# Cached pages on 16 neighbouring partitions with eight rows each, in place of 32 partitions four apart with four rows

## The reference, cut to what matters

```
def diff_core(q1, q2, k1, k2, v, lam, q_pos, k_pos):
    s1 = einsum('bqhd,bkhd->bhqk', q1, k1) * scale      # masked where k_pos > q_pos
    s2 = einsum('bqhd,bkhd->bhqk', q2, k2) * scale
    p1 = softmax(s1); p2 = softmax(s2)
    return einsum('bhqk,bkhd->bqhd', p1 - lam * p2, v)

cache_k_diff  (1, N_PHYS, 128, 4 heads, 128)   paged rotated [k1|k2]
cache_v_diff  (1, N_PHYS, 128, 4 heads, 128)   paged values
page_table    (8 sequences, 16 pages)
```

## Time and profile before

| | us |
|---|---|
| median of 3 runs | 1942.77 (1932.91 to 1943.87) |
| the profiled execution | 1937.89 |
| its span in the profile | 1935.9 |

### The profile page before, as it was taken

How to read it: one execution, slowest core, us unless ns; L and a number is a source line. 1 busy time by engine, 2 the same in 40 slices (tenths; PEclk the granted TensorE clock), 3 DMA queues, 4 the chain that set the end, 5 groups by cost and what they waited for, 6 DMA issues and landing times.

```text
span 1935.9 us, 32623 instructions
## 1 busy us (share of the span) xinstructions
PE 1621.9 (84%) x12772; PEld 770.8 (40%) x12772; DVE 695.8 (36%) x1351; ACT 331.3 (17%) x769; POOL 214.0 (11%) x356
## 2 busy tenths in 40 slices
PE   7999888888897978877787879998978888877784
PEld 3444455555444323222232357764532222223231
DVE  4446578867515200000000169973250000000005
ACT  3100344444302000000000020013110000000001
POOL 1000223322201110110100040000021101011000
PEclk9999999988898998999999989999979999999998
DMA  9995699989754999999999999922279999999995
GB/s 336 358 361 191 230 335 355 364 319 354 298 212 166 368 428 428 412 428 428 427 428 427 390 314 324 320 102 126 87 275 427 426 415 426 426 428 427 428 424 203
DMA packets 83829, 659.20 MB, mean 341 GB/s; under 512 B 15307, under 2 KB 15436, under 8 KB 45418
## 3 DMA queue, kind: packets, MB, share of 16 engines
q1 hardware_dynamic: 58906, 569.86, 74.0%
q0 software_dynamic: 24800, 87.65, 11.9%
HBM read 643.18 MB, written 96.53 MB: 382 GB/s over the span
## 4 chain that ended last, share of the span: by engine, by line
PE 50%; DMA 35%; DVE 9%; issue 3%; ACT 2%; SPq 1%; DVEq 0%; ACTq 0%; POOLq 0%
DMA ring<-in 32%; PE ps L2294 14%; PE ps L2249 7%; PE ps L2457 6%; PE ps L1874 6%; PE ps L1838 3%; PE ps L2063 2%; DMA ring<-y_rows 2%; PE ps L2478 2%; DVE ring L1283 2%; PE ps L2048 1%; DVE ring L1276 1%; PE ps L2314 1%; DMA out<-x 1%; PE ps L2003 1%
## 5 line engine op out<-in xcount | busy, mean ns | idle before, releaser
L2294 PE MATMUL ps<-ring,big 128*32 128x512 f32 (+1 forms) x2688 | 471.5, 649 | 135.9 <-DMA ring<-in 130.0
L2294 PEld LDWEIGHTS ps<-ring,big 128*32 128x32 f32 (+1 forms) x2688 | 146.4, 131 | 456.5 <-issue 390.1
L1555 DVE TENSOR_TENSOR big<-big,ps 128x512 f32<-128x512 f32 x32 | 22.0, 688 | 822.5 <-PE ps L2294 777.6
L2314 PE MATMUL ps<-ring,big 128*32 128x512 f32 (+1 forms) x928 | 214.0, 602 | 17.5 <-ACT big L797 12.3
L797 ACT ACTIVATE big<-ps 128x512 f32<-128x512 f32 (+6 forms) x166 | 84.3, 517 | 826.1 <-PE ps L1838 527.1
L2249 PE MATMUL ps<-ring,big 128*128 128x512 f32 (+1 forms) x288 | 123.4, 610 | 5.7 <-ACT big L1191 4.8
L2457 PE MATMUL ps<-act_t,ring 128*128 128x288 f32 x512 | 124.4, 406 | 0.0
L2314 PE MATMUL ps<-act_t,big 128*32 128x512 f32 (+1 forms) x416 | 99.0, 594 | 15.4 <-ACT big L797 10.5
L2457 PEld LDWEIGHTS ps<-act_t,ring 128*128 128x128 f32 x512 | 97.2, 190 | 26.8
L1779 DVE SCALAR_TENSOR_TENSOR big<-big,par 128x512 f32<-128x512 f32 x240 | 103.9, 510 | 0.0
L1874 PE MATMUL ps<-ring,act_t 128*128 128x512 f32 x208 | 96.9, 614 | 5.7 <-DMA ring<-in 4.4
(11 more groups left out here) (322 smaller groups left out, 1761.3 us busy)
## 6 DMA issues: line engine op xcount, KB each, us to landing
ring<-in SPq DMA_DIRECT2D x180, 2048.0 KB, 18.3
out<-in SPq DMA_DIRECT2D x16, 4080.0 KB
ring<-in SPq DMA_DIRECT2D x128, 256.0 KB, 7.0
ring<-in POOLq DMA_DIRECT2D x128, 256.0 KB, 7.3
act_t<-in SPq DMA_DIRECT2D x16, 2048.0 KB
ring<-in SPq DMA_DIRECT2D x28, 1024.0 KB, 10.2
ring<-in SPq DMA_DIRECT2D x24, 512.0 KB, 6.2
ring<-in POOLq DMA_DIRECT2D x24, 512.0 KB, 5.0
```

Of the source, the lines that this page charges most:

```text
L2294: ins = mm(ps[half, i, :], XgT[:, par_, k, half], slot(eslots(w)[i], 8)[:, k, :], start=(k == 0), stop=(k == KC - 1))
L2314: ins = mm(ps[half, 5 + h, :], hbT[:, k, half], down_weights(w, odd)[:, k, h * 512:(h + 1) * 512], start=(k == 0), stop=(k == 3))
```

## The change

A page goes to 16 neighbouring partitions, and takes eight rows in each: 16 pieces of 16 KB in place of 32 of 8 KB. Page j lies on partitions 16*(j%8) to 16*(j%8)+15 and there in rows 8*(j//8) to 8*(j//8)+7, so that eight pages in a row, not four, fill a stretch of rows in every partition. Keys and values are moved alike. Number and order of the transfers, their bytes, their queues and their semaphores stay. Since rows 0 to 3 now hold something of each of pages 0 to 7, `turn_pages` waits for both semaphores before the even quarter, and not before the odd one.

```
     def pages_in(eng, pages, first, src, dst, arrived):
 
         for j, page in enumerate(pages, first):
-            held = dst[j % 4::4, j // 4 * 4:j // 4 * 4 + 4, :].rearrange("p n c -> p (n c)")
-            rows_of = src[bass.ds(page, 1)].rearrange("a (p e) c -> (a p) (e c)", e=4)
+            held = dst[16 * (j % 8):16 * (j % 8) + 16, j // 8 * 8:j // 8 * 8 + 8, :].rearrange("p n c -> p (n c)")
+            rows_of = src[bass.ds(page, 1)].rearrange("a (p e) c -> (a p) (e c)", e=8)
             eng.dma_start(held, rows_of).then_inc(arrived[j // 4], 16)
@@
             keys = Kd[:, 4 * k:4 * k + 4, :].rearrange("p n c -> p (n c)")
-            dve.wait_ge(kd_in[k], X_TILE[k] + 64 * (b + 1))
+            if k % 2 == 0:
+                for i in (k, k + 1):
+                    dve.wait_ge(kd_in[i], X_TILE[i] + 64 * (b + 1))
             V.transpose(keys, keys).then_inc(kd_turned, 1)
```

## The result

| | before | changed |
|---|---|---|
| median, us | 1943.87 (1932.91 to 1946.98, 5 runs) | 2184.76 (2150.5 to 2191.3, 5 runs) |
| the profiled execution, us | 1937.89 | 2170.67 |
| its span, us | 1935.9 | 2168.6 |
| ratio to before | 1 | 1.1131 (95% interval 1.1084 to 1.1179) |

The changed kernel is 11.3% slower; this ratio leaves out three of its five runs, which lie over 1.5% above its fastest one, and so it is smaller than that of the medians, 1.124. The forecast had said slower, 2087 us, in a range of 1960 to 2330 us: direction and range hold. The median lies 98 us above it; the profiled execution lies 89 us above the 2082 us that the sum gave for it.

The account below looks back on a forecast made before the run. PE, DVE and ACT bound the attention stage, with DMA just keeping up; pages 349, window rows 93 and tail 19 make it 461 us, +141, and +3 for sequence 0 gives 2082 us profiled, 2087 us median, range 1960 to 2330 us.

Parts of the forecast that it names:

- The bound of before: Attention stage: PE, DVE and ACT set its length, DMA just keeps up; faster transfers bring at most 14 us.
- Fewer, larger pieces bring nothing: Page transfers: 16 KB pieces gain nothing per byte; taken as 0, from the bounds 0 and -14 us.
- The wait for eight pages: DVE's turns at 14 places: 0 to 32 us if the transfer rate stays; taken as 0.
- Sequence 0: Its key pages, moved during the projection: third turn some 3 us late, +3 us, bounds 0 and +16.
- The price of a byte: Pages on 16 neighbours: keys (SP) at 147 GB/s, 200 us; values (POOL) at 225 GB/s, 149 us.
- The window rows: Attention stage: 39.3 MB of window rows moved at 422 GB/s, 93 us.
- The reserve of 59 us: Attention stage before: what 320 us leave after 242 us of transfer and 18.7 us of tail.
- the tail of 19: End of the attention stage: 18.7 us after the last pages land that transfers can't cover.
- Strong contention: Rival: a page's 16 pieces hold each other up, pages under 150 GB/s, 2155 to 2330 us; chance 0.27.
- the likeliest case: Attention stage: pages at 150 to 260 GB/s, +34 to +211 us, 1975 to 2155 us; chance 0.55.
- No contention that matters: Rival: engines drift apart, pages above 302 GB/s fit the reserve, 1943 to 1958 us; chance 0.15.
- Each engine owns some partitions: Rival: few engines carry each page at full speed, at most 35 us; chance counted in halves to two other cases.

Follow-up runs that it names:

- The values alone: Only the values' pages laid on 16 neighbouring partitions, keys as in the kernel before: 2065.59 us, ratio 1.0658 to before.
- the order of the stretches: Changed kernel with a batch's pages sent to stretches in order 0, 1, 4, 5, 2, 3, 6, 7: 2144.77 us; 0, 2, 1, 3, 4, 6, 5, 7: 2226.73 us.
- the keys alone: Only the keys' pages laid on 16 neighbouring partitions, values as in the kernel before: 2083.8 us, ratio 1.0743 to before.

## Why the prediction was right, and where it was off

**The bound of before, and "a slower transfer is felt soon".** Right. The stage alone grew, by 232.4 us, and its longest waits are DMA. The signs named in advance came: DMA share near 1, GB/s down, pages of SP landing after 19.2 us, 4096 packets fewer (79733).

**Fewer, larger pieces bring nothing.** Right as to the rate. SP's issue of a page did get cheaper (316 ns in the median where it took 472), and it bought nothing. Nor are the fewer pieces what made it cheaper: 32 neighbours with before's 32 pieces also took 316 ns, and 16 pieces eight apart took 496.

**The wait for eight pages, put at 0.** Right: ratio 0.9986 alone.

**Sequence 0, +3 us.** Too much. Its turns start at 177.73 and 188.03 us (177.59 and 187.89 before). Those pages started to move near 154 us, not 163, the last of them ended at 177.9 us, ten before the third turn, and coming on one queue alone they moved faster than the 147 GB/s that I had taken (1012 ns a packet, 259 GB/s of engine time). The window shows all that moves:

```profile
165.00:175.00 10.00, 10.00 (x30) 4.17 (x27) 8.50 (x12) 1.57 (x3) 1.80 (x3) 1.00 0.96 246
```

**The price of a byte: the right place, both prices off.** That 16 neighbours are held up at the destination is shown by the kernels with the same pieces elsewhere. The terms: for keys I took 147 GB/s (200 us) and they had 29.4 MB / 176 us = 167; for values 225 GB/s (149 us) and they had 33.6 MB / 199 us = 168. Pages cost 375 us where the sum had 349: 24 too much for the keys and 50 too little for the values. The mis-sized term is that of POOL's queue: its x tile had been held up less than SP's y tile, I took this for a trait of the queue, and it isn't. The values alone, for which the forecast's price leaves at most 25 us, cost 126. That the keys' price came near is luck. It was taken from a tile on 64 partitions with packets 2.9 times as long as at full rate, but pages on 64 neighbours, the kernel that is like it, take only 1.6 times as long on either queue, and 16 neighbours 2.5 times. "I let these cancel" had no row behind it. What slowed that tile more was not taken apart.

**The window rows, put at 93 us.** Too little, and this is the larger error: 134 us, +41. Two things are in it. Some 14 us were there before the change: 93 us is the peak rate, and window rows already took some 107 us of engine time. The other 27 us are new. Their packets go to all 128 partitions, yet those of 4 KB took 227 ns (POOL) and 234 ns (SP) where before 180 and 192, and those of 8 KB 392 and 438 where before 320 and 338, pages among them. That narrow pages slow whatever moves beside them was nowhere in my sum. With only the keys narrow, the 8 KB packets on POOL's queue, four fifths of them values laid out as before, took 377 ns in place of 320 too.

**The reserve of 59 us and the tail of 19.** Together they claim 78 us without transfers; the engines of before are idle for 38 us. I had set transfers at the peak rate, 242 us, while the earlier trace rows say that the engines are busy 0.88 of 320 us, 282 us. Besides the slower packets, 12 us of them are 4.2 MB of weights of the next stage, and some 6 us are small packets and instructions; the sum had neither (in the changed kernel 12 and 11 us). After the change the engines are idle for 20 us, and that this looks like my tail of 19 is luck: only 6 of them lie at the end, behind the last page (754.3 us), and 10 lie between 628 and 648 us, where the share is 0.50.

So: 375 of pages + 134 of window rows + 12 of weights + 11 of small and instruction packets + 20 idle = 552 us, against 349 + 93 + 19 = 461 us in the forecast. The missing 91 us are 26 + 41 + 12 + 11 + 1. About a third, 14 + 12 + 6 = 32 us, was engine time of the kernel before that my sum had left out; the rest is the price of narrow pages, on themselves and on what moves beside them.

**The rivals.** "Strong contention" began at 150 GB/s; the pages had 168, at the strong end of the likeliest case, but the time of 2185 us lies past that case's 2155 us and within the strong one's, by what the window rows and the terms left out added. So the case that I held likeliest is right in its rate and not in its time. "No contention that matters" wants 302 GB/s and is out. "Each engine owns some partitions" is out too: packets themselves took 2.5 times as long, which they wouldn't if each engine carried pieces at full speed. That engines drift apart would fit the order of the stretches, which moves 82 us.

## What to carry to other kernels

Lay a transfer out so that it alone reaches all 16 ports as the table above counts them: 16, 32 and even 64 neighbours cost 1.6 to 3.1 times the engine time of the same bytes at full rate, where 32 partitions four apart, 64 two apart or all 128 cost 1.03 to 1.11 times, whatever the size of the pieces. Where narrow transfers can't be avoided, let consecutive ones go to stretches that share no port in that count, and count what moves beside them as slowed too. Take the reserve of a stage from the busy share in its window, not from bytes over the peak rate.

## What the runs showed that I had not expected

**The clock of TensorE.** PE's 5217 instructions of the stage were busy 311.5 us at a granted clock of 0.74, where 5216 were busy 272.4 us at 0.92. With waits of 16 to 50 us for pages between them, stretches run at the lower of its two levels (1.2 in place of 2.4 GHz). The page scores of the last sequence show it: PE had stood idle for 13.8 us, started them at a clock of 0.50, and had 1.00 again in the window from 740 us on:

```profile
725.00:730.00 5.00, 0.00 (x0) 0.00 (x0) 2.92 (x2) 0.00 (x0) 0.00 (x0) 0.50 1.13 419
730.00:735.00 5.00, 3.27 (x64) 1.06 (x65) 3.73 (x11) 1.45 (x7) 0.00 (x0) 0.50 1.01 166
735.00:740.00 5.00, 4.86 (x89) 2.43 (x72) 1.07 (x1) 0.82 (x4) 0.00 (x0) 0.71 1.06 184
740.00:750.00 10.00, 6.90 (x142) 5.07 (x140) 4.73 (x21) 6.14 (x20) 0.00 (x0) 1.00 0.96 298
```

```profile
731.73 7.07 PE L2065 MATMUL ps<-ring 32*16 32x512 f32 x128 [13.79 <-DVE ring L1285]
```

Since the DMA engines are idle for only 20 us of the stage, the 39 us can't have made it longer by more than a part of these 20; how much of them is on the chain I did not separate.

**TensorE stops for nothing that the profile shows.** With the keys alone narrow, the chain holds more "issue" than in any other kernel, 16.0% of 459 us against 9.3% of 320 us before. One such piece, in the midst of 32 page products, 9 of which were done:

```profile
357.46 8.60 issue
```

```profile
366.07 1.48 PE L2134 MATMUL ps<-ring,act_t 128*16 128x128 f32 x23 [8.60 <-issue]
```

In that stretch one packet of instructions came through, among the pieces of the narrow pages:

```profile
q8 instruction: 1, 0.02, 1.1%
```

Its record has it from 362.82 to 364.66 us; PE went on 1.4 us later. The pause isn't the only one of its kind. In the stage of this kernel PE is idle 17 times for over 3 us, and 12 of these pauses end 1.25 to 1.77 us after the end of an instruction packet of 16 KB that came within the pause. There are 42 such packets in 464 us, so that chance would give about one. With the kernel before there is one pause of over 3 us in the stage, and its instruction packets take 0.98 us in the mean, not 1.30. That PE waited there for its own instructions fits the times closely. That the packets came late because they stood behind pages is argued; no run took it apart. Nor do the pauses explain why the keys alone lose more than half: the DMA engines are busy for 443 of 464 us of that stage, so that it is the slower packets that make it long. Why narrow key packets took 1899 ns with wide values beside them and 1572 ns with narrow ones isn't settled.
